# The scan's output matmuls of a group's eight heads in one burst, their evictions and the gate two units later

## The reference

```
proj = x @ w_in                                  # z, xbc, dt
xbc = silu(causal_depthwise_conv(xbc, conv_w, conv_b))      # xs, bm, cm
dt = softplus(dt + dt_bias); a = -exp(a_log)
decay = exp(segsum(dt * a))                      # per head, 256 x 256, causal
cb = einsum('bclgn,bcsgn->bgcls', cc, bc)        # per group
y_diag = einsum('bgcls,bgrcls,bcsgrp->bclgrp', cb, decay, xs * dt)
y = y_diag + d_skip * xs
yg = y * silu(z)
yg = yg * rsqrt(mean(yg * yg over the group) + eps) * norm_g
return yg @ w_out
```

## Time and profile before

| | us |
|---|---|
| median of 3 runs | 2423.49 (2423.23 to 2424.59) |
| the profiled execution | 2423.12 |
| its span (first to last instruction) | 2421.9 |
| PE busy | 2410.3 |
| DVE busy | 1571.3 |
| ACT busy | 1242.8 |
| POOL busy | 89.6 |

### The profile page before, as it was taken

The page is one execution under the profiler, slowest core; times in us unless marked ns, Lnnn a source line. Parts: engine busy times, 40 slices in busy tenths (PEclk is TensorE's granted clock), DMA queues, the critical chain, the costliest instruction groups (busy, mean ns, idle before and its releaser), DMA issues.

```text
span 2421.9 us, 45332 instructions
## 1 busy us (share of the span) xinstructions
PE 2410.3 (100%) x19568; PEld 2333.9 (96%) x19568; DVE 1571.3 (65%) x2105; ACT 1242.8 (51%) x1427; POOL 89.6 (4%) x68
## 2 busy tenths in 40 slices
PE   9999999999999999999999999999999999999998
PEld 9999999999999999999988899999999999999998
DVE  6778888865577766665575556656655555555556
ACT  5446665654364565554464445445444445455463
POOL 0001000100031000000000000000000000000002
PEclk9999999999999999999999999999999999999999
DMA  7666666657755655547757666666655576655645
GB/s 249 198 194 186 207 189 187 184 185 247 233 165 165 192 166 149 161 151 242 223 192 240 196 197 195 193 185 196 183 190 188 189 237 206 183 172 175 190 158 183
DMA packets 262969, 467.37 MB, mean 193 GB/s; under 512 B 16433, under 2 KB 66161, under 8 KB 260849
## 3 DMA queue, kind: packets, MB, share of 16 engines
q1 hardware_dynamic: 262624, 464.21, 62.2%
q10 hardware_dynamic: 144, 0.26, 0.0%
HBM read 451.64 MB, written 4.26 MB: 188 GB/s over the span
## 4 chain that ended last, share of the span: by engine, by line
PE 97%; DVE 1%; DMA 1%; ACT 1%; issue 0%; ACTq 0%
PE G L676 91%; PE M L676 5%; PE M L689 1%; DMA RAW<-in_ssd_w_in 1%; DVE W L1521 0%; DVE BT L1550 0%; DVE W2m L1521 0%; DVE W0m L1521 0%; DVE E L1606 0%; ACT W0m L1088 0%; DVE E L1647 0%; DVE SZ L1677 0%; DVE E L1608 0%; DVE BT L1543 0%; DVE W L1512 0%
## 5 line engine op out<-in xcount | busy, mean ns | idle before, releaser
L676 PE MATMUL G<-AA,W 128*128 128x256 f32 x7892 | 935.5, 277 | 2.7 <-DVE W L1521 1.6
L676 PEld LDWEIGHTS G<-AA,W 128*128 128x128 f32 x7892 | 913.1, 188 | 8.2 <-issue 3.8
L1521 DVE TENSOR_TENSOR W<-RAW,W 128x1024 fp32r<-128x1024 f32 (+1 forms) x443 | 553.0, 1250 | 359.1 <-ACT W L1088 358.0
L1088 ACT CAST W<-RAW 128x1024 fp32r<-128x1024 f32 (+1 forms) x443 | 461.4, 1047 | 453.1 <-PE G L676 438.8
L676 PE MATMUL G<-AA,WY 128*128 128x256 f32 x2508 | 304.2, 277 | 0.0
L676 PEld LDWEIGHTS G<-AA,WY 128*128 128x128 f32 x2508 | 293.0, 188 | 1.7 <-issue 1.4
L1521 DVE TENSOR_TENSOR WY<-RAW,WY 128x1024 fp32r<-128x1024 f32 (+1 forms) x112 | 140.9, 1260 | 72.9 <-ACT WY L1088 72.8
L676 PE MATMUL G<-W0m,YY 128*128 128x256 f32 x1512 | 183.7, 276 | 0.4 <-DVE W0m L1521 0.2
L676 PE MATMUL G<-W1m,YY 128*128 128x256 f32 x1512 | 182.9, 276 | 0.1
L676 PE MATMUL G<-W,YY 128*128 128x512 f32 x792 | 181.3, 389 | 0.0
L676 PE MATMUL G<-W2m,YY 128*128 128x256 f32 x1488 | 180.4, 276 | 0.0
(11 more groups left out here) (304 smaller groups left out, 2389.8 us busy)
## 6 DMA issues: line engine op xcount, KB each, us to landing
RAW<-in_a_w_in SPq DMA_DIRECT2D x192, 512.0 KB, 4.0
RAW<-in_ssd_w_in SPq DMA_DIRECT2D x160, 512.0 KB, 4.5
RAW<-in_b_w_in SPq DMA_DIRECT2D x128, 512.0 KB, 4.2
RAW<-in_dsa_w_in SPq DMA_DIRECT2D x72, 512.0 KB, 3.7
RAW<-in_ssd_w_out SPq DMA_DIRECT2D x64, 512.0 KB, 4.8
RAW<-in_dsa_w_out SPq DMA_DIRECT2D x64, 512.0 KB, 4.4
RAW<-in_a_w_out SPq DMA_DIRECT2D x64, 512.0 KB, 3.7
RAW<-in_b_w_out SPq DMA_DIRECT2D x32, 512.0 KB, 4.1
```

What stands on the lines that cost most here:

```text
L676: return e.matmul(o, l, r, start=start, stop=stop, skip_group_check=True)
L1088: e.copy(wh[:, 0:n], RAW[:, v % NR, 0:n]).then_inc(*up(cast_done, "cast", v))
L1521: e.tensor_tensor(wl[:, 0:n], RAW[:, v % NR, 0:n], wh[:, 0:n].bitcast(F), ALU.subtract).then_inc(*up(rest_done, "rest", v))
```

## The change

The two bursts become one. On PE the wait for XD moves ahead of the loop, `ssd` waits five steps instead of three, and both halves (heads 0 to 3 and 4 to 7) are issued in step 17. On DVE two more `yield` stand ahead of the four evictions, which are now in steps 17 to 20. `gate_z` starts 4 units late (2 for g = 0), on all engines. Nothing else is changed; the line numbers behind the first hunk of the tensor program are lower by 3 or 1.

```diff
@@ walk
             run(("x", g), ("ssd", g))
-            run(("z", g), later(0 if g == 0 else 2, "gate_z", g))
+            run(("z", g), later(2 if g == 0 else 4, "gate_z", g))
@@ tensor_program, ssd
                 last.then_inc(*up(pe_made, "xd_t", g, t))
                 yield
-            yield
-            yield
-            yield
+            for _ in range(5):
+                yield
+            e.wait_ge(*on("read", "xd", g, 1))
             for i in range(2):
                 b = take("ty", g, i)
-                if i == 0:
-                    e.wait_ge(*on("read", "xd", g, 1))
                 e.wait_ge(*on("em", g, i))
...
                 last.then_inc(*up(pe_made, "y_m", g, 2 * i + 1))
-                yield
-                yield
+            yield
```

## The result

The changed kernel takes **2451.61 us** (median of 4 runs, 2450.69 to 2453.1) against 2423.68 before (4 runs): **ratio 1.0116, 95% interval 1.0105 to 1.0128**. It is slower by 28 us, where 8 were forecast, and outside the range. The profiled execution took 2453.1, with a span of 2451.8.

A forecast was written before the change was run, and what follows sets the result against it. PE, 97% of the chain, bounds the kernel; afterwards the DVE, GpSimd, ACT loop does. Distances +0.6, 5 x 1.2 = +6.0, last +1.9, saving -0.4: +8.1 us, 2431.6 us from the median; range 2425.5 to 2437.

The forecast's parts named there:

- 0.41 saved per group: On PE: one merged burst of 3.09 us replaces two of 1.75, saving 0.41 a group, 3.3 in eight.
- the walk: Loop DVE, GpSimd, ACT, DVE between CB products of heads 4 to 7: 50.3 us, group 50.35 instead of 49.15.
- 20.0: From the end of the decays to the next group's CB product: 18.75 us before, net +1.28, 20.0 in all.
- SP's queue keeps its order; no DMA moves.: SP's DMA queue: order unchanged and no transfer moves; no cost was counted.
- GpSimd's product ... takes 2.43: GpSimd's product behind the last eviction: starts 0.14 later, takes 2.43 us, done at 17.7 in the loop.
- Rival 4: GpSimd slows DVE's subtractions, about 1 us more in five or six distances: +13.6, 2437.1 us; chance 10%.
- I take half, +0.6: First distance between bursts: more in hand, no gate in front of group 0, so half of +1.2, +0.6 us.
- PE's next five units are already cast while the five tiles turn: Casts behind the later Square, held 3 to 5 us: costed at nothing; without this cover up to 2 us a group.
- the sign that the cover was wrong: PE waiting for subtractions (DVE W) in the middle groups would show the cover of five tiles was wrong.
- Rival 5: PE's clock falls to the 1.2 GHz level for a unit behind each wait: +19 on the forecast, 2450.6 us; chance 2%.

The follow-up runs named there:

- e2: Kernel before with the merged burst, evictions two a step in steps 17 and 18, gate as before: 2424.33 us, ratio 1.0002.
- e9: e2 with GpSimd's product cut in two halves, the first waiting for the first two evictions only: 2421.56 us, ratio 0.9992.
- e3: Changed kernel with the CSB transfer issued three steps earlier, in step 3 of the scan instead of step 6: 2437.51 us, ratio 1.0055.
- e5: Kernel before with the gate two units later and evictions in steps 17 to 20, its two bursts left apart: 2448.98 us, ratio 1.0109.
- e4: Changed kernel with its evictions two a step in steps 17 and 18, gate still two units later: 2428.03 us, ratio 1.0017.
- e14: e11 with the CSB transfer issued three steps earlier: 2425.08 us, ratio 1.0006.
- e13: e10 with the CSB transfer issued three steps earlier: 2430.97 us, ratio 1.0030.
- e10: Changed kernel with GpSimd's product cut in two halves: 2442.26 us, ratio 1.0076.
- e12: Kernel before with GpSimd's product cut in two halves and nothing else: 2423.36 us, ratio 0.9999.
- e11: Changed kernel with its evictions in three steps, 17 (two), 18 and 19, the last one a step earlier: 2430.6 us, ratio 1.0027.
- e7: e4 with the CSB transfer issued three steps earlier: 2432.2 us, ratio 1.0033.
- e8: e4 with the gate two units later for groups 0 to 4, one for group 5, as before for the last two: 2430.65 us, ratio 1.0028.

## Why the prediction was wrong, and where right

**The burst's saving, right.** "0.41 saved per group": measured 0.445 (e2, e9: 49.145 - 48.70). The estimate by the page of the Trainium skill (FP8 and Floating Point Precision, TensorE Precision Notes) was 0.47; the measured value lies between.

**The mechanism, right in the main.** The loop that the walk named sets the pace, through the named releaser: PE waits for DVE at the CB product's line, and GpSimd's product, Square, the casts, the reciprocal and the decays follow each other without slack. Only between cast and reciprocal the chain runs through DVE's own subtractions (in e3 they end at 402.64, the Sqrt at 402.24), not through the Sqrt. e5 shows that the merged burst has hardly a part in it, e4 and e14 that the step of the last eviction does, e13 that it is a loop. "20.0" from the decays to the next CB product was 19.9.

**The step that failed first: "SP's queue keeps its order; no DMA moves."** The order did stay, and that was the trouble: a transfer in a queue of unchanged order moves when what stands ahead of it moves. SP's fetches wait for DVE's subtractions, those for casts behind Square. The walk moved DVE by microseconds and left SP where it was. The transfer had had 8.2 to 9.4 us from issue to first use against a median landing of 8.5, no reserve at all: DVE waited 0.7 us for it in all. In the changed kernel it is issued 4.3 us later in the loop, it lands 6.1 to 8.9 us behind that, and the first decay waits for it in all seven groups, 13.3 us in all. It cost 14.1 us (e3), half of all.

**The second: "GpSimd's product ... takes 2.43".** It took 3.27 to 3.32 in the first six groups. The row was of another neighbourhood: before, the last eviction stood ahead of four convolution steps, after it stands ahead of a subtraction. Rival 4 named the pair of engines but looked for the harm on DVE, in the folds. The product's part is 0.85 in each group that waits for it: five or six, 4 to 5 us. With it the walk gives 51.2, and e3 measured 51.21, 51.23 and 51.22.

**The first distance: "I take half, +0.6"** was -0.26, and -0.45 in e3: the first groups have reserve enough, and the saving of the burst counts there in full. A term too high by about 1 us.

**The covers: "PE's next five units are already cast while the five tiles turn".** This failed in three of the five middle stretches of the changed kernel, by waits for weights of 1.4, 2.00 and 3.83 us; the prediction had named such waits as the sign that the cover was wrong. In e3, e10, e13, e14 and e4 one unit alone waits there, the last in front of the sixth stretch's burst: 3.30, 4.27, 2.52, 1.50 and 2.06 us. With the loop's length alone it doesn't go: e10's loop is shorter than the changed kernel's, and its wait is longer. The text priced it at up to 2 us a group; it was more in the sixth stretch, and 2.54 us in the output projection behind it. What makes this weight late was not sorted out.

**Rival 5, "the clock falls (2%)",** was too sure of itself on a row of the first 20 us, and it misread them. The column shows 1.00, but PE's first matmuls are these:

```profile
1.58 5.01 PE L676 MATMUL M<-ident 128*128 128x128 f32 x28 [1.58 <-POOL ident L2286]
```

Their starts are 0.213 us apart up to 4.9 us and 0.112 apart behind it, so the lower level was there; behind the idle times of 0.47 and 0.55 us that follow, the pace stays. In the changed kernel the granted clock is 0.94 between 410 and 470 us. Five stretches of 11 to 22 matmuls run at the 1.2 GHz level, at 0.21 us a matmul instead of 0.113, behind waits of 2.00 to 3.83 us: together about 8 us, where the rival had 19. The Trainium skill, TensorE: Matmul & The Clock Gate, A second HAM failure mode, does let short idle times cost clock; the trace agrees for some waits and not for others: two of 2.26 and 2.71 us in the same kernel, and four of 1.7 to 2.0 in front of the second halves of e3's bursts, had no such stretch behind them.

**The sum.** The distances grew by 375.5 - 345.2 = 30.3 us. By the profile of after: -3.1 for seven merged bursts, +20.2 of PE's listed waits (9.8 for the CB product, 10.4 for weights, of which before had 0.2), about +8 for the clock. That makes 25. Of the other 5, the same waits take 1.5 more when they are counted from start to start of the matmuls (21.7), and the rest is intervals of 0.15 to 0.4 us between two matmuls, most of them right behind a wait or at the edge of a half-clock stretch. By the runs: 14.1 with the CSB transfer (e3), 12.4 more down to e14 (the eviction's step, its product, and the weights and the clock behind them), and 1.8 that e14 still has over before.

## What to carry to other kernels

An instruction that keeps its place in its queue still moves when anything ahead of it waits longer. So when a walk delays one engine, follow it into the DMA queue that waits for that engine, and compare the time from issue to use with the time from issue to landing. Take a duration from a row with the same neighbour on the other engine, not only the same shape. And look at what stands behind the last event of a loop: beside the merged burst, cutting the product in two gave 2.8 us (e2 to e9), where the merged burst alone had given none and the cut alone none (e12).

## What the runs showed that I had not expected

**Two engines, one at a time.** GpSimd's product and DVE's subtraction RAW less W never ran side by side at full speed. Where the product starts 0.22 us behind a subtraction (396.79 and 397.01 in the changed kernel), it takes 3.28 us and the subtraction its 1.22. Where the subtraction comes second, the product keeps 2.43 and the subtraction takes 2.18 or 2.19 (e11). The convolution steps beside it, XG<-G,VC,XG, take 0.47 each as ever. The Trainium skill, SBUF — State Buffer, Who interferes with whom, has it so: a DVE instruction with two SBUF inputs contends with one of GpSimd's that reads SBUF, and the order of issue decides which of them is held; the trace agrees, in all six long products of after and of e3.

**Half the clock behind a wait.** A unit behind waits of 3.83 and 3.30 us for a weight took 5.46 us, twice its 2.72, at a granted clock of 0.50; behind one of 2.52 it took 4.59 (e13), behind 1.50 it took 3.01 (e14), and behind 2.84 it took 3.00 (e8). So a late weight costs its wait and up to 2.7 us more, and the length of the wait alone doesn't decide it. What does was not tried.

**Less waiting asked for, more time.** e7 and e8, each e4 with an edit meant to take a wait away, were 4 and 3 us slower than it. In a schedule with this little reserve an edit is worth what a run says.
